# Score blocks of the recurrent stage: 32 by 32 diagonal pieces in place of whole 128 by 128 products

## The chip, the cores and the metric

The kernel runs on one core of a Trainium2 chip. Its time is the device time of one execution in microseconds (us). TensorE (PE in the profile, PEld for its weight loads) multiplies, VectorE (DVE), ScalarE (ACT) and GpSimd (POOL) do the rest, SyncE (SP) issues the transfers.

## The reference

One layer of an encoder: 1024 tokens and 16 meta tokens, width 1024. A projection feeds two branches, latent attention and a bidirectional gated recurrence (HGRN2, 8 heads of 128 channels); they are merged by gates, projected, and a SwiGLU feed-forward layer follows. The change lies in the recurrence. In short form, for one head and one direction, with the decays `g` summed up to `b` within a chunk:

```python
b = jnp.cumsum(g_c, axis=2)
q_r = q_c * exp(b - b_ref)            # b_ref: a reference point near the query
k_r = k_c * exp(b_ref - b)
a = einsum('td,sd->ts', q_r, k_r)     # scores inside the chunk
a = where(causal, a, 0.0)
o = a @ v_c + (q_c * exp(b)) @ S      # S: the state before the chunk
S = exp(b_last) * S + (k_c * exp(b_last - b)).T @ v_c
```

The reference point has to be near both positions, or the exponents grow too far. So the scores of a chunk are made in blocks, each with a reference of its own. Both directions are made and added.

## The kernel before

The stage of the recurrence, `hgrn_heads`, goes through the 8 heads. Its chunks have 128 tokens (`CH`), and it works on groups of 512 tokens (`HALF`, 4 chunks, `GC`). TensorE's program is software-pipelined: `project` makes the projections of the next head (13 outputs `e` of 8 steps `k` of three matmuls each, lines 88 to 90), and the list `PE_STEPS` says after which of these steps, numbered `e * 8 + k`, a piece of the current head's recurrence is put in:

```python
PE_STEPS = [(36, "turn", 0), (38, "turn", 1), (39, "updates", 0), (40, "turn", 2), (42, "updates", 1),
            (43, "turn", 3), (45, "turn", 4), (47, "updates", 2), (51, "inside", 0), (53, "updates", 3),
            (57, "updates", 4), (60, "inside", 1), (66, "outputs", 0), (71, "inside", 2), (75, "norm_sum", 0),
            (78, "inside", 3), (85, "outputs", 1), (90, "norm_sum", 1)]
```

ACT and DVE have such lists too (`ACT_STEPS`, `DVE_STEPS`). Every engine runs its own list in order, and semaphores tie them together. DVE's list has, in this order around the change: `factors_multiply` 0 (lines 822 and 825: the decay factors times queries and keys), `states` 2 (line 845), weight 3 (line 895), `factors_multiply` 1, `states` 3, `keep` 0, `factors_subtract` 2 (lines 797 to 802), `states` 4, `keep` 1, weight 4, `factors_subtract` 3, `factors_multiply` 2 and 3, `keep` 2.

`inside(h, i)` makes the scores of one direction and one group of 4 chunks, i = 0 to 3. It waits for `fac_done` (DVE's `factors_multiply` i) and for `kept` (DVE's `keep` i - 1 has read the bank), and writes `in_bank`, one PSUM bank of 128 partitions (keys) by 4 times 128 columns (queries):
- 4 matmuls of 128 by 128 (line 958), one for each chunk, with the factors `k32` and `q32`, whose references lie in the middle of every 32 tokens. Only the 32 by 32 blocks on the diagonal of these products are of use.
- 4 matmuls of 64 by 64 and 8 of 32 by 32 (line 967) for the blocks off the diagonal, which write over what the first 4 left there. For one direction the 64-wide ones all go to the same half of the partitions; the 32-wide ones go to partitions 0 and 64 in turn (forward) or 32 and 96 (backward).

The operands are fp32. Each such matmul stands in the trace as two pairs of a weight load and a matmul (two passes). `keep` then picks the valid triangle by a mask (`copy_predicated`). `updates` i waits for `ends_copied` and for `state_done` (DVE's `states` i - 1 has read the bank `u_bank`). The printed functions follow.

Of the kernel before, what the change touches and what calls it, by code (L numbers as in the profile page):

```python
# [43 lines left out]
CH = 128  # L44
NCH = SEQ // CH
SUB = 32
QUARTER = D // 4
HALF = 512
GC = HALF // CH
# [449 lines left out]
def hgrn_heads(nc, t, hn_hi, hn_lo, weights):  # L499
# [9 lines left out]
    with ExitStack() as c:  # L509
        def sb(name, shape, dt=F32):  # L510
            return c.enter_context(nc.sbuf_tensor(name, shape, dt))
# [5 lines left out]
        q, gate = sb("q", [P, SEQ]), sb("gate", [P, SEQ])  # L517
# [19 lines left out]
        ends_bank, in_bank, o_bank, u_bank = bank[4:8]  # L537
# [17 lines left out]
        zeroed, masks_filled, masks_made = t.sem("zeroed"), t.sem("masks_filled"), t.sem("masks_made")  # L555
# [21 lines left out]
        def place(dd, name, g=0):  # L577
            a = {"q64": 0, "k64": 256, "q128": 512, "k128": 768, "q32": 1024, "k32": 1536, "q0": 2048 + g * HALF}[name]
            n = 256 if name in ("q64", "k64", "q128", "k128") else HALF
            return factor[dd][:, a:a + n]  # L580
# [4 lines left out]
        with nc.Block() as block:  # L585
# [50 lines left out]
            def _(act):  # L636
                def sigmoids(h, _):

                    proj_copied.wait(act, h, N_PROJ)
                    q_done.wait(act, h, 1, lag=1)  # L640
                    kept.wait(act, h, 4, lag=1)
                    r_done.wait(act, h, 4, lag=1)
                    for n in IN_HGRN:
                        dst = {"q": q, "hg": gate}.get(n, raw[n])
                        act.activation(dst[:], raw[n][:], ACT.Sigmoid).then_inc(sig_done.sem, 1)
                    act.preload_act_table_set("natural_log_exp_and_others")
                    for dd, n in ((FWD, "ff"), (BWD, "fb")):
                        sig_done.wait(act, h, dd + 1)
                        hh = h.index() + dd * HEADS
                        act.activation(sub[dd][:], raw[n][:], ACT.Ln, bias=t.lb[:, bass.ds(hh, 1)],  # L650
                                       scale=t.omlb[:, bass.ds(hh, 1)]).then_inc(g_done.sem, 1)
# [85 lines left out]
            def _(dve):  # L737
# [150 lines left out]

                dve.wait_ge(masks_made, 1)
                dve.wait_ge(zeroed, 2)  # L890

                def weight_lo(p, s):

                    w_hi_done.wait(dve, p, s + 1)
                    dve.tensor_tensor(w_lo[s % 2][:], w_raw[s % 2][:], w_hi[s % 2][:].bitcast(F32),  # L895
                                      ALU.subtract).then_inc(w_lo_done.sem, 1)
# [16 lines left out]
            def _(pe):  # L913
# [34 lines left out]
                def inside(h, i):  # L948

                    dd, g = GROUPS[i]  # L950
                    fac_done.wait(pe, h, i + 1)
                    if i:
                        kept.wait(pe, h, i)
                    else:
                        kept.wait(pe, h, 4, lag=1)
                    for u in range(GC):
                        a = slice(u * CH, (u + 1) * CH)
                        pe.matmul(in_bank[:, a], place(dd, "k32")[:, a], place(dd, "q32")[:, a], start=True,
                                  stop=True)
                    for span in (128, 64):  # L960
                        half = span // 2
                        for n in range(HALF // span):
                            u, at = n * span // CH * CH, n * span % CH
                            keys = at + (0 if dd == FWD else half)
                            queries = u + at + (half if dd == FWD else 0)
                            b = slice(n * half, (n + 1) * half)
                            last = pe.matmul(in_bank[keys:keys + half, queries:queries + half],
                                             place(dd, f"k{span}")[:, b], place(dd, f"q{span}")[:, b],
                                             start=True, stop=True)
                    last.then_inc(in_done.sem, 1)  # L970

                def outputs(h, g):
# [22 lines left out]
                def project(p, h, s):  # L995

                    made = projections(p)
                    w_lo_done.wait(pe, p, s + 1)
                    for i, (a, w) in enumerate(made.chunks[s]):
                        e = made.first(s) + i  # L1000
                        same = [x for x in range(e) if made.banks[x] == made.banks[e]]
                        if same:
                            proj_copied.wait(pe, p, same[-1] + 1)
                        else:
                            last_use = max(x for x in range(N_PROJ) if OF_HEAD.banks[x] == made.banks[e])
                            proj_copied.wait(pe, p, last_use + 1, lag=1)
                        out = bank[made.banks[e]][:, 0:w]
                        for k in range(KT):
                            last = three(pe, out, w_hi[s % 2][:, k, :], w_lo[s % 2][:, k, :], hn_hi[:, k, a:a + w],
                                         hn_lo[:, k, a:a + w], k == 0, k == KT - 1)  # L1010
                            if k == KT - 1:
                                last.then_inc(proj_done.sem, 1)
                            if h is not None:
                                for at, name, j in PE_STEPS:
                                    if at == e * KT + k:
                                        steps[name](h, j)

                steps = {"turn": turn, "updates": updates, "inside": inside, "outputs": outputs,
                         "norm_sum": norm_sum}

                def both(p, h):
                    if h is not None and h.j is None and h.base == 0:
                        pe.wait_ge(zeroed, 2)
                    for s in range(6):
                        project(p, h, s)

                iterations(pe, both)


# [1958 lines left out]
```

## Time and profile before

| what | value |
|---|---|
| time of 3 runs | 2173.63, 2174.02 (median), 2174.09 us |
| span of the profiled execution, first to last instruction | 2171.4 us |
| what lies around the span (median minus span) | 2.6 us |
| stage of the recurrence | about 126 to 906 us of the span |
| calls of `inside` | 32 (8 heads by 4) |

The time that is compared is the one of the runs; stretches are read from the profiled execution, whose time is taken as its span and the 2.6 us around it. A matmul's duration in the trace is longer than its distance to the next one, since matmuls overlap: what a matmul costs is read from the distance of starts. Weight loads (PEld) overlap matmuls as well.

### The profile page before, as it was taken

The page shows a single profiled execution, that of the slowest core. Times are in us where ns is not written, and L with a number is a line of the kernel's source. Part 1 is how long each engine was busy: PE and PEld are TensorE (multiplying, and loading weights), DVE is VectorE, ACT ScalarE, POOL GpSimd, SP SyncE. Part 2 cuts the span into 40 slices and gives each one's busy share as a digit, 9 for nine tenths or more (in the row PEclk, how much of TensorE's full clock was granted, in tenths as well). Part 3 has the DMA queues.
Part 4 walks back from the last instruction along what each step waited for, and adds up shares of the span by engine and source line. Part 5 has one row for each costly group of instructions (what it writes and reads, how often), then busy time and mean ns, then how long its engine had stood idle before and what let it go on. Part 6 is the DMA issues. An engine that isn't in the chain of part 4 may idle for free. (4 is left out here: it accounts for less than half of the span.)

```text
span 2171.4 us, 30857 instructions
## 1 busy us (share of the span) xinstructions
PE 2124.8 (98%) x11536; PEld 1795.8 (83%) x11536; DVE 1282.6 (59%) x1966; ACT 948.0 (44%) x1550; POOL 397.9 (18%) x242
## 2 busy tenths in 40 slices
PE   8999999999999999999999999899999999999999
PEld 8988888888888888778888888777888888888886
DVE  3403664756647557447777777667866766651431
ACT  6314354443554535455555555545432323243422
POOL 1110000000000000021111111020065554524443
PEclk9999999999999999999999999999999999999999
DMA  5112111120120111130111111254322222354452
GB/s 188 60 54 69 35 64 53 45 68 34 63 68 34 63 52 46 49 138 1 45 45 48 47 50 47 99 186 159 135 83 81 95 78 73 124 182 165 149 182 96
DMA packets 79101, 181.82 MB, mean 84 GB/s; under 512 B 6976, under 2 KB 27776, under 8 KB 77344
## 3 DMA queue, kind: packets, MB, share of 16 engines
q1 hardware_dynamic: 79008, 180.56, 24.1%
q8 instruction: 61, 1.00, 0.2%
q14 instruction: 32, 0.26, 0.0%
HBM read 142.13 MB, written 38.40 MB: 83 GB/s over the span
## 5 line engine op out<-in xcount | busy, mean ns | idle before, releaser
L88 PE MATMUL h_bank<-hn_hi,w_hi 128*128 128x512 f32 (+2 forms) x952 | 371.1, 390 | 2.8 <-ACT raw L716 1.6
L90 PE MATMUL h_bank<-hn_hi,w_lo 128*128 128x512 f32 (+2 forms) x952 | 353.4, 371 | 0.0
L89 PE MATMUL h_bank<-hn_lo,w_hi 128*128 128x512 f32 (+2 forms) x952 | 353.0, 371 | 0.0
L88 PEld LDWEIGHTS h_bank<-hn_hi,w_hi 128*128 128x128 f32 x952 | 179.0, 188 | 33.3 <-issue 8.7
L90 PEld LDWEIGHTS h_bank<-hn_hi,w_lo 128*128 128x128 f32 x952 | 178.7, 188 | 27.9
L89 PEld LDWEIGHTS h_bank<-hn_lo,w_hi 128*128 128x128 f32 x952 | 179.2, 188 | 26.4 <-issue 3.8
L716 ACT COPY raw<-h_bank 128x512 f32<-128x512 f32 (+2 forms) x119 | 63.9, 543 | 279.9 <-PE h_bank L90 249.5
L2150 ACT CAST w_hi<-w_raw 128x1024 fp32r<-128x1024 f32 x79 | 82.8, 1049 | 213.2 <-PE f_bank L90 201.7
L895 DVE TENSOR_TENSOR w_lo<-w_raw,w_hi 128x1024 fp32r<-128x1024 f32 x52 | 63.5, 1221 | 138.2 <-ACT w_hi L696 138.2
L1132 POOL MEMSET ckv_hi<- 128x224 f32 x1 | 0.3, 284 | 778.8 <-POOLq L585 778.8
L1453 ACT CAST prob_hi<-a_bank 128x512 fp32r<-128x512 f32 x144 | 83.0, 588 | 130.8 <-PE a_bank L1721 130.2
L2120 POOL TENSOR_TENSOR w_lo<-w_raw,w_hi 128x1024 fp32r<-128x1024 f32 x45 | 108.3, 2406 | 144.5 <-ACT w_hi L2150 144.5
L88 PE MATMUL f_bank<-ffn_in_hi,w_hi 128*128 128x512 f32 x320 | 126.7, 396 | 2.1 <-DVE w_lo L2439 1.3
L90 PE MATMUL f_bank<-ffn_in_hi,w_lo 128*128 128x512 f32 x320 | 124.6, 389 | 0.0
L89 PE MATMUL f_bank<-ffn_in_lo,w_hi 128*128 128x512 f32 x320 | 124.5, 389 | 0.0
L2125 POOL TENSOR_TENSOR set_lo<-combos,set_hi 128x512 fp32r<-128x512 f32 x72 | 98.7, 1372 | 87.2 <-ACT set_hi L2213 87.2
L88 PE MATMUL f_bank<-t_hi,set_hi 128*128 128x512 f32 x288 | 112.0, 389 | 0.0
L89 PE MATMUL f_bank<-t_lo,set_hi 128*128 128x512 f32 x288 | 112.0, 389 | 0.0
L90 PE MATMUL f_bank<-t_hi,set_lo 128*128 128x512 f32 x288 | 112.0, 389 | 0.0
L1572 DVE TENSOR_TENSOR prob_lo<-a_bank,prob_hi 128x512 fp32r<-128x512 f32 x144 | 97.7, 688 | 24.0 <-ACT prob_hi L1453 20.3
L2213 ACT CAST set_hi<-combos 128x512 fp32r<-128x512 f32 x72 | 44.5, 618 | 99.8 <-PE f_bank L90 64.9
L88 PE MATMUL f_bank<-t_hi,w_hi 128*128 128x512 f32 x224 | 87.7, 391 | 0.0
(411 smaller groups left out, 5371.3 us busy)
## 6 DMA issues: line engine op xcount, KB each, us to landing
w_raw<-in_w_ffn SPq DMA_DIRECT2D x82, 512.0 KB, 3.7
w_raw<-in_w_hgrn SPq DMA_DIRECT2D x54, 512.0 KB, 3.2
raw_up<-in_w_ffn SPq DMA_DIRECT2D x18, 512.0 KB, 4.6
hidden<-gate_blocks SPq DMA_DIRECT2D x34, 256.0 KB, 2.0
w_raw<-in_w_out SPq DMA_DIRECT2D x15, 512.0 KB, 3.3
w_raw<-in_w_head SPq DMA_DIRECT2D x9, 512.0 KB, 6.0
X<-in_x SPq DMA_DIRECT2D x8, 520.0 KB, 9.4
values<-values_h SPq DMA_DIRECT2D x32, 128.0 KB, 1.7
```

The lines of the kernel that those rows point to most:

```text
L88: pe.matmul(out, wh, xh, start=start, stop=False)
L89: pe.matmul(out, wh, xl, start=False, stop=False)
L90: return pe.matmul(out, wl, xh, start=False, stop=stop)
L716: act.copy(t.raw[:, s * L + a:s * L + a + w], bank[made.banks[e]][:, 0:w]).then_inc(proj_copied.sem, 1)
L895: dve.tensor_tensor(w_lo[s % 2][:], w_raw[s % 2][:], w_hi[s % 2][:].bitcast(F32), ALU.subtract).then_inc(w_lo_done.sem, 1)
L1132: pool.memset(part[:, :, L:].bitcast(F32), 0.0).then_inc(padded, 1)
L1453: act.copy(turned_hi[k % RING][:], turn_bank[k % 2][:]).then_inc(p_hi.sem, 1)
L1572: dve.tensor_tensor(turned_lo[k % RING][:], turn_bank[k % 2][:], turned_hi[k % RING][:].bitcast(F32), ALU.subtract).then_inc(p_lo.sem, 1)
L2120: pool.tensor_tensor(w_lo[b % 2][:], w_raw[b % 2][:], w_hi[b % 2][:].bitcast(F32), ALU.subtract).then_inc(w_lo_done, 1)
L2125: pool.tensor_tensor(set_lo[:, i], product_source(mat, i), set_hi[:, i].bitcast(F32), ALU.subtract).then_inc(set_lo_done, 1)
L2150: act.copy(w_hi[b % 2][:], w_raw[b % 2][:]).then_inc(w_hi_done, 1)
L2213: act.copy(set_hi[:, i], product_source(mat, i)).then_inc(set_hi_done, 1)
```

## The change

The 4 whole products go. In their place, at the end of `inside`, stand 16 matmuls of 32 by 32 for the blocks on the diagonal; they go to partitions 0, 32, 64 and 96 in turn. The 4 matmuls of 64 by 64 and the 8 of 32 by 32 off the diagonal stay and come first, so a call of `inside` now issues 4 + 8 + 16 = 28 fp32 matmuls (56 passes) where it issued 4 + 4 + 8 = 16 (32 passes). The semaphore `in_done` is raised by the last of the 16. Blocks of the bank that nothing writes any more (below or above the diagonal) are set to zero once, by DVE, before the loop; TensorE waits for that before the first head of the recurrence.

```diff
                 dve.wait_ge(zeroed, 2)
+                dve.memset(in_bank[:], 0.0).then_inc(zeroed, 1)
...
-                    for u in range(GC):
-                        a = slice(u * CH, (u + 1) * CH)
-                        pe.matmul(in_bank[:, a], place(dd, "k32")[:, a], place(dd, "q32")[:, a], start=True,
-                                  stop=True)
                     for span in (128, 64):
                         half = span // 2
...
-                            last = pe.matmul(in_bank[keys:keys + half, queries:queries + half],
-                                             place(dd, f"k{span}")[:, b], place(dd, f"q{span}")[:, b],
-                                             start=True, stop=True)
+                            pe.matmul(in_bank[keys:keys + half, queries:queries + half],
+                                      place(dd, f"k{span}")[:, b], place(dd, f"q{span}")[:, b],
+                                      start=True, stop=True)
+                    for n in range(HALF // SUB):
+                        at, b = n * SUB % CH, slice(n * SUB, (n + 1) * SUB)
+                        last = pe.matmul(in_bank[at:at + SUB, b], place(dd, "k32")[:, b], place(dd, "q32")[:, b],
+                                         start=True, stop=True)
                     last.then_inc(in_done.sem, 1)
...
-                        pe.wait_ge(zeroed, 2)
+                        pe.wait_ge(zeroed, 3)
```

## Rows read from the trace of the kernel before

**Rows 1.** The page: span, busy time of the engines, share, instructions.

```profile
span 2171.4 us, 30857 instructions
PE 2124.8 (98%) x11536; PEld 1795.8 (83%) x11536; DVE 1282.6 (59%) x1966; ACT 948.0 (44%) x1550; POOL 397.9 (18%) x242
```

**Rows 2.** Recurrence stage: length, busy PE, PEld, DVE, ACT, POOL, granted clock, DMA.

```profile
126.00:906.00 780.00, 775.40 (x4712) 662.23 (x4712) 446.27 (x780) 343.48 (x499) 1.68 (x4) 1.00 0.16 52
```

**Rows 3.** TensorE's waits over the span: who for whom, total us, times, longest.

```profile
PE h_bank L958 <- DVE factor_f L825: 1.9, 8, 0.3
```

**Rows 4.** Timeline of TensorE around `inside` 1, second head: start, length, instruction.

```profile
326.72 0.39 PE L90 MATMUL h_bank<-hn_hi,w_lo 128*128 128x512 f32 x1
326.95 1.05 PE L958 MATMUL h_bank<-factor_b 128*128 128x128 f32 x8
327.93 1.05 PE L967 MATMUL h_bank<-factor_b 128*64 128x64 f32 x24
328.92 0.50 PE L88 MATMUL h_bank<-hn_hi,w_hi 128*128 128x512 f32 x1
329.25 0.39 PE L89 MATMUL h_bank<-hn_lo,w_hi 128*128 128x512 f32 x1
```

**Rows 5.** The same call in narrow windows: last whole pass, 64-wide, 32-wide passes.

```profile
327.73 0.28 PE L958 MATMUL h_bank<-factor_b 128*128 128x128 f32 x1
...
327.93 0.68 PE L967 MATMUL h_bank<-factor_b 128*64 128x64 f32 x8
...
328.54 0.45 PE L967 MATMUL h_bank<-factor_b 128*32 128x32 f32 x16
```

**Rows 6.** Groups by line and form, 220 to 890 us: busy us, mean ns.

```profile
L967 PE MATMUL h_bank<-factor_b 128*64 128x64 f32 x128 | 10.9, 228 | 0.0
...
L967 PE MATMUL h_bank<-factor_b 128*32 128x32 f32 x256 | 7.1, 199 | 0.0
```

**Rows 7.** Timeline of DVE and TensorE around `inside` 0, second head.

```profile
316.08 0.68 DVE L825 TENSOR_TENSOR factor_f<-factor_f,key_f 128x512 f32<-128x512 f32 x1
...
316.81 1.16 PE L958 MATMUL h_bank<-factor_f 128*128 128x128 f32 x8 [0.26 <-DVE factor_f L825]
...
317.90 1.05 PE L967 MATMUL h_bank<-factor_f 128*64 128x64 f32 x24
...
318.88 0.50 PE L88 MATMUL h_bank<-hn_hi,w_hi 128*128 128x512 f32 x1
```

**Rows 8.** Timeline of DVE from weight 3 to `keep` 0, second head.

```profile
317.70 1.22 DVE L895 TENSOR_TENSOR w_lo<-w_raw,w_hi 128x1024 fp32r<-128x1024 f32 x1
...
321.38 0.68 DVE L825 TENSOR_TENSOR factor_b<-factor_b,key_b 128x512 f32<-128x512 f32 x1
321.98 1.49 DVE L845 SCALAR_TENSOR_TENSOR state<-state,decay,h_bank 128x128 f32<-128x128 f32 x4
323.40 0.75 DVE L876 COPY_PREDICATED scores<-consts,h_bank 128x512 f32<-128x512 uint32 x1
```

**Rows 9.** Timeline of the weight loads: the first load of `updates` 4.

```profile
323.78 0.19 PEld L944 LDWEIGHTS h_bank<-values_h,ends_t 128*128 128x128 f32 x1
```

**Rows 10.** ACT's copy before `updates` 2; TensorE's sequencer at line 83 in 310.36:310.70.

```profile
309.75 0.59 ACT L665 COPY ends_t<-h_bank 128x512 f32<-128x512 f32 x1 [1.39 <-PE h_bank L927]
...
L83 PEldq ALU_OP  x1: 32/32/32, 310.4 to 310.4; - x1
```

**Rows 11.** Timelines of DVE, ACT and TensorE between `inside` 1 and `inside` 2.

```profile
329.12 0.06 DVE L864 MEMSET waited<- 128x1 f32 x1 [2.04 <-PE h_bank L967]
...
331.29 0.59 ACT L716 COPY raw<-h_bank 128x512 f32<-128x512 f32 x1 [6.91 <-PE h_bank L90]
...
336.98 0.69 DVE L825 TENSOR_TENSOR factor_f<-factor_f,key_f 128x512 f32<-128x512 f32 x1
...
339.23 0.49 PE L958 MATMUL h_bank<-factor_f 128*128 128x128 f32 x3
```

**Rows 12.** Timeline of DVE: its first instruction of the stage.

```profile
138.93 1.22 DVE L895 TENSOR_TENSOR w_lo<-w_raw,w_hi 128x1024 fp32r<-128x1024 f32 x1 [44.52 <-ACT w_hi L696]
```

## The prediction, made before the changed kernel was run

> **What bounds the kernel now.** The page comes first: TensorE is busy 98% of the span, DVE 59%, ACT 44% [rows 1]. Then the stage of the recurrence by itself: TensorE is busy 775.4 of 780 us at a granted clock of 1.00, which is the level of 2.4 GHz [rows 2]. So time comes off only where TensorE's own work shrinks, and only as long as nobody else becomes late. The list of waits shows who is nearly late: `inside` 0 of each head waits for DVE's `factors_multiply` 0, 8 times, 1.9 us in all [rows 3]. Busy time is no price here, because neighbours on TensorE overlap; prices come from distances between starts in the timeline. I read them in one head; the groups have one mean duration over the stage [rows 6].
>
> **One call of inside, now.** In `inside` 1 the first whole product starts at 326.95 and the projection goes on at 328.92: 1.97 us. The starts split it into 0.98 (8 passes of whole products), 0.61 (8 passes 64 wide) and 0.38 (16 passes 32 wide) [rows 4, 5]. Subtracting one duration from the end of a group gives its last start:
> - whole products: last start 327.73, so (327.73 - 326.95) / 7 = 0.111 a pass, then 0.20 to the first 64-wide start;
> - 64 wide: end 328.61, less 0.22 is 328.39, so 0.46 / 7 = 0.066 a pass, then 0.15;
> - 32 wide: end 328.99, less 0.20 is 328.79, so 0.25 / 15 = 0.0167 a pass, then 0.13 [rows 5, 6].
>
> The 0.20, 0.15 and 0.13 are stops at a change of the matmul's form.
>
> **Removed.** The 8 whole passes with their stop, 0.98 us. A new stop takes their place, from the projection's 512 columns to the 64-wide form. No row shows it. After a whole pass 0.20 go by, of which its 128 columns stream for 0.05 at 2.4 GHz; 0.15 follow the stream. A projection matmul streams 512 columns in 0.21, and the next one starts 0.23 after it [rows 4]. So the stop adds 0.21 + 0.15 - 0.23 = about 0.13; I take 0.135, with 0 (hidden) and 0.20 (the whole distance) as its bounds.
>
> **Added.** 16 matmuls, 32 passes, 32 wide, behind the 16 passes of that form that stay. No further change of form. What counts is their pace, and whether it is that of the 16 old ones depends on where they go. The 64-wide matmuls of one call all go to one half of the partitions and take 0.066 a pass. The 32-wide ones alternate between two column groups. Half the columns should take half of that, 0.033; the row has 0.0167 [rows 5]. I read this as two groups working side by side, each at 0.033 a pass. The new ones go round four groups. If four work side by side, groups 0 and 64 (or 32 and 96) have 16 passes each, 8 old and 8 new, and set the end: 15 x 0.033 + 0.02 for the stagger of the groups = 0.52 from first to last start. I take this, as the nearest reading of the rows. If only two ever work side by side, it is 47 x 0.0167 = 0.785.
>
> By the Trainium skill (TensorEngine Tiling (Array Packing), Key Properties) different tiles load weights and multiply in parallel; this supports four, and would give the 0.52. The trace shows two. The same notes speak against the change elsewhere: TensorE: Matmul & The Clock Gate, section "Wait — 56ns, not 53.3ns?", says that start to start is never below about 25 ns, however few the columns. The trace has 17 ns over 16 passes; whether it holds over 48 no row shows, and that is a rival below.
>
> Can the sequencer issue so many? Behind the wait of `turn` 4, which ACT's copy ends at 309.75 + 0.59 = 310.34, stand 20 weight loads and matmuls (`turn` 4 and two steps), then the wait of `updates` 2, whose sequencer operation is there at 310.4 [rows 10]: 0.1 us at most for 20, 5 ns each. 48 passes are 96 instructions, 0.48 us, under the 0.52. So issue doesn't bind, though with little to spare.
>
> **A call of inside, after.** 0.135 + 0.61 + 0.52 + 0.13 = 1.395 us, so 1.97 - 1.395 = 0.575 saved in `inside` 1, 2 and 3.
>
> **Inside 0 is different.** There the engine is idle before it, so no stop at the front: from 316.81 to 318.88 are 2.07 now [rows 7], after it 0.61 + 0.52 + 0.13 = 1.26, 0.81 saved. But it can't be kept. `updates` 4, six steps later, waits for `states` 3. DVE works without a gap from `factors_multiply` 0 through weight 3, `factors_multiply` 1 and `states` 3, which ends at 321.98 + 1.49 = 323.47 [rows 8]. It doesn't wait for TensorE in that stretch, so it won't be earlier. TensorE's first load of `updates` 4 is at 323.78 [rows 9]; a load follows DVE's end by about 0.05 (316.76 to 316.81, [rows 7]), so it could be at 323.52. Of the 0.81, 0.26 are kept and 0.55 become a wait at `updates` 4. The wait before `inside` 0 stays at 0.26: what leads to it is unchanged.
>
> **Is anything else late after that?** TensorE reaches `inside` 2 earlier by 0.26 + 0.575 = 0.84. Its factors are ready at 336.98 + 0.69 = 337.67, its first product starts at 339.23 with the load 0.23 ahead: 1.3 to spare [rows 11]. And that DVE work moves along: DVE sits idle until `inside` 1 ends, and ACT's copy is released by the projection [rows 11]. So the rest is kept.
>
> **The rest.** The memset on DVE is one instruction of 128 x 512, priced by the nearest row on the same bank at 0.75 [rows 8]; DVE is idle until 138.93, for 44.52 us [rows 12]: nothing. Without that cover it would be 0.75 once. The wait for `zeroed` comes a head later: nothing.
>
> **The sum.** A head gives 0.26 + 3 x 0.575 = 1.985, 8 heads 15.9 us. The profiled execution is 2171.4 + 2.6 = 2174.0, the median of the runs. 2174.0 - 15.9 = 2158.1.
>
> **Rivals.**
> - *Two groups at a time.* For it: it is the only pace in the rows. Against: nothing in them says that two is the limit. A call takes 0.135 + 0.61 + 0.785 + 0.13 = 1.66, saves 0.31; `inside` 0 would save 0.545, keeps 0.26. A head: 1.19, in all 9.5: 2164.5.
> - *A slower pace in a long burst.* The short burst of now may live on what is already queued, and a longer one fall to a slower pace. I price it half way between the 0.0167 of two groups and the 0.033 of one, at 0.025 for the new passes: 0.25 + 32 x 0.025 + 0.13 = 1.18; a call 1.925, saves 0.045; a head 0.26 + 3 x 0.045 = 0.395, in all 3.2: 2170.8, no change that a measurement tells. Against: the 5 ns of issue. The 25 ns of the Trainium skill (TensorE: Matmul & The Clock Gate, the section named above) would come to this.
> - *Neighbouring groups don't overlap* (slower). The rows show only groups two apart, 0 and 64 or 32 and 96; the new order takes 0, 32, 64, 96. If each pass has to wait for its neighbour: 0.25 + 32 x 0.033 + 0.13 = 1.436; a call 2.18, loses 0.21; `inside` 0 keeps 0.02. A head loses 0.61, in all 4.9: 2178.9. It decides from the pace at which a head breaks even: three calls may lose 0.087 each, so 32 passes may take 1.97 + 0.087 - 0.745 - 0.38 = 0.93, 0.029 a pass. At the 0.066 of the 64-wide ones it would be over 30 us slower.
> - *Everything is given back*: TensorE waits elsewhere, DVE or ACT setting the length of a head. For it: DVE already holds two places in each head. Against: the 1.3 us at `inside` 2, and that DVE is released by TensorE there. It gives 2174.
>
> **How the numbers follow.** Four side by side 0.55, two 0.23, the slower pace 0.08, no overlap of neighbours or worse 0.10, all given back 0.04. The forecast is the first, 2158. The first two hold 0.78, so the range reaches to the third, 2171. Its low end: with the stop at the front hidden, 3 x 0.135 x 8 = 3.2 less, 2154.9, and a little of what I let be lost at `updates` 4; 2154. A measurement of this kernel tells 0.2%, 4.3 us, from no change: 2169.7 and 2178.4. So faster 0.78, same 0.12 (slower pace and all given back), slower 0.10.
>
> **What would show it.** Right: line 958 is gone; the 32-wide group of a call takes about 0.5 us from first to last start; a call lasts about 1.4; the waits show `updates` 4 (line 944) waiting for DVE's line 845, about 0.5 us in each head, and nothing new before `inside` 1 to 3; granted clock stays 1.00. Wrong: 32-wide starts 0.025 or 0.033 apart; a stop between old and new 32-wide ones; or a stop at the front beyond 0.20. The pace of the new passes is the step most likely to fail.

## The result, and the profile after

The changed kernel takes 2158.15 us (2157.74 to 2158.28); the kernel before took 2174.06 beside it. The ratio is 0.9926, with a 95% interval of 0.9912 to 0.9939: 0.7% less, which is small but clear of the noise. The prediction was 2158.0, range 2154 to 2171. The number is met; the parts below show that two of its terms were off and that a third, unforeseen cost made up for them. Times are medians; one execution of the last version below took 10,700 us at a granted clock of 0.18, and its time is given without it.

The page of the kernel after, which answers to [rows 1]: span, busy time, instructions.

```profile
span 2156.3 us, 32394 instructions
PE 2108.2 (98%) x12304; PEld 1771.7 (82%) x12304; DVE 1283.3 (60%) x1967; ACT 948.1 (44%) x1550; POOL 397.3 (18%) x242
```

The stage of the recurrence, as in [rows 2], from its first matmul to the end of its last:

```profile
126.69:888.82 762.13, 756.20 (x5480) 637.50 (x5480) 445.86 (x781) 343.52 (x498) 1.64 (x4) 1.00 0.16 53
```

It was 779.8 us long from its first matmul (126.09) to the end of its last (905.91) and is 762.1 now: 17.7 less, at the same granted clock of 1.00. The span is only 15.1 shorter (2171.4 less 2156.3). So 2.6 us were lost outside the stage; they come up again below.

TensorE's timeline around `inside` 1 of the second head, which answers to [rows 4]. The projection before the call ends in the first line, and it resumes in the last but one.

```profile
324.76 0.39 PE L90 MATMUL h_bank<-hn_hi,w_lo 128*128 128x512 f32 x1
325.08 0.96 PE L964 MATMUL h_bank<-factor_b 128*64 128x64 f32 x18
325.85 0.22 PE L969 MATMUL h_bank<-factor_b 128*32 128x32 f32 x1
325.87 0.23 PE L964 MATMUL h_bank<-factor_b 128*32 128x32 f32 x3
325.90 0.22 PE L969 MATMUL h_bank<-factor_b 128*32 128x32 f32 x2
...
325.96 0.45 PE L969 MATMUL h_bank<-factor_b 128*32 128x32 f32 x28
326.34 0.50 PE L88 MATMUL h_bank<-hn_hi,w_hi 128*128 128x512 f32 x1
326.67 0.40 PE L89 MATMUL h_bank<-hn_lo,w_hi 128*128 128x512 f32 x1
```

And in a narrow window, as in [rows 5], the first of the 32-wide passes:

```profile
325.69 0.29 PE L964 MATMUL h_bank<-factor_b 128*32 128x32 f32 x6
```

Three things are to be seen. From the last projection matmul to the next one are 326.34 - 324.76 = 1.58 us, where it was 328.92 - 326.72 = 2.20 [rows 4]: 0.62 saved. The 48 passes 32 wide run from 325.69 to 325.96 + 0.45 - 0.20 = 326.21: 0.52 us for 47 steps, 0.011 a pass. And the first new matmuls (line 969) start between old ones (line 964) that stand ahead of them in the program, so they didn't wait for all of the old ones.

The same for `inside` 0, with its wait in brackets, and the place where `updates` 4 begins; they answer to [rows 7] and [rows 9]:

```profile
315.21 1.02 PE L964 MATMUL h_bank<-factor_f 128*64 128x64 f32 x21 [0.22 <-DVE factor_f L825]
...
316.47 0.50 PE L88 MATMUL h_bank<-hn_hi,w_hi 128*128 128x512 f32 x1
...
321.36 0.39 PE L90 MATMUL h_bank<-hn_hi,w_lo 128*128 128x512 f32 x1
321.92 1.16 PE L945 MATMUL h_bank<-values_h,ends_t 128*128 128x128 f32 x8 [0.17 <-DVE state L845]
322.83 0.48 PE L88 MATMUL h_bank<-hn_hi,w_hi 128*128 128x512 f32 x1
```

TensorE's waits, as in [rows 3]: the second line and the third are new. The third belongs to the feed-forward part.

```profile
PE h_bank L964 <- DVE factor_f L825: 1.9, 8, 0.3
...
PE h_bank L945 <- DVE state L845: 1.5, 8, 0.3
...
PE f_bank L88 <- POOL w_lo L2121: 0.9, 1, 0.9
```

DVE's `states` 3 in the same head, as in [rows 8]:

```profile
320.38 1.49 DVE L845 SCALAR_TENSOR_TENSOR state<-state,decay,h_bank 128x128 f32<-128x128 f32 x4
```

It ends at 321.87, and `updates` 4 (line 945 now) starts at 321.92. The list gives this wait 1.5 us in all, 0.19 a head, since a matmul's modelled end covers part of it; what it costs is seen in the starts. Matching the projection's matmuls of the two kernels one by one (the nth of line 88 with the nth), the changed kernel's TensorE gains 0.78 to 0.84 us at `inside` 0, loses 0.42 to 0.50 again at `updates` 4, and gains 0.59 to 0.62 at each of `inside` 1 to 3. In the second head the last two are 0.44 and 3 x 0.62.

### The profile page after: what moved, and what is told of

Same layout as the page of the kernel before. It is cut to its first block and busy times, and to the rows that moved or that the text cites. A ratio compares the mean times of both kernels' runs of the same rounds, so it can differ in the third digit from the quotient of the medians.

```text
span 2156.3 us, 32394 instructions
## 1 busy us (share of the span) xinstructions
PE 2108.2 (98%) x12304; PEld 1771.7 (82%) x12304; DVE 1283.3 (60%) x1967; ACT 948.1 (44%) x1550; POOL 397.3 (18%) x242
## 3 DMA queue, kind: packets, MB, share of 16 engines
q8 instruction: 63, 1.03, 0.2%
```

## The experiments

A column group is here the set of 32 partitions of the PSUM bank (0, 32, 64 or 96 and the 31 behind it) to which a 32-wide matmul writes. Where one time is given, the kernel ran once; the kernel before, beside it, took 2173.34 us with the first three, 2174.33 (median of seven) with the order by chunk and the three better versions, and 2174.02 with the last two. The executions of one kernel scatter by 1 to 2 us, so small differences are read from stretches of the trace and not from these times.

**Do column groups work side by side?** Three kernels send the 16 new matmuls of a call elsewhere. They multiply the factors `k64` and `q64`, so that the bank holds bounded numbers; the scores on the diagonal are left out. The first sends all to one group:

```diff
-    at, b = n * SUB % CH, slice(n * SUB, (n + 1) * SUB)
-    last = pe.matmul(in_bank[at:at + SUB, b], place(dd, "k32")[:, b], place(dd, "q32")[:, b],
+    at, b, c = 0, slice(n * SUB, (n + 1) * SUB), slice(n % 8 * SUB, (n % 8 + 1) * SUB)
+    last = pe.matmul(in_bank[at:at + SUB, b], place(dd, "k64")[:, c], place(dd, "q64")[:, c],
```

> The 16 new matmuls of a call all write partitions 0 to 31, with the factors k64 and q64 in place of k32 and q32, so the blocks on the diagonal are not computed. Theory (column groups work side by side, each at about 0.032 us a pass): forward calls have 8 + 32 = 40 passes in group 0, 1.27 us from the first to the last 32-wide start, instead of 0.52; backward calls 32 there, 1.0 to 1.3 us. A head gets 2.1 to 2.6 us longer (0.43 of inside 0 is taken up by the wait at updates 4), the kernel 17 to 21: 2175 to 2179. Rival (a pace by the number of instructions, wherever they go): 0.52 us as now, 2158.

The others have `at = n % 2 * 64` and `at = n % 2 * SUB`.

> The 16 new matmuls go to partitions 0 and 64 in turn (factors k64 and q64, blocks on the diagonal not computed). Theory (each group 0.032 us a pass): forward calls have 24 passes in each of two groups, 0.76 us from first to last 32-wide start; backward calls, whose old ones go to 32 and 96, between 0.52 (old and new side by side) and 0.76. 2160 to 2164. Rival (pace by number): 0.52, 2158.

> The 16 new matmuls go to the neighbours 0 and 32 in turn (factors k64 and q64, blocks on the diagonal not computed). Theory: neighbours overlap like groups two apart, forward 24 passes in group 0, 0.76 us, 2160 to 2164, as with 0 and 64. Rival (neighbours share a path): 0.25 + 32 x 0.033 = 1.3 us, about 2176.

They took 2176.40, 2161.19 and 2161.84 us, all three as the theory has it. The timelines of `inside` 0 in the second head, all to one group:

```profile
317.90 1.05 PE L964 MATMUL h_bank<-factor_f 128*64 128x64 f32 x24 [0.26 <-DVE factor_f L825]
318.79 1.18 PE L969 MATMUL h_bank<-factor_f 128*32 128x32 f32 x32
319.89 0.50 PE L88 MATMUL h_bank<-hn_hi,w_hi 128*128 128x512 f32 x1
```

and in turn to groups 0 and 64:

```profile
315.19 1.05 PE L964 MATMUL h_bank<-factor_f 128*64 128x64 f32 x24 [0.26 <-DVE factor_f L825]
316.07 0.68 PE L969 MATMUL h_bank<-factor_f 128*32 128x32 f32 x32
316.68 0.50 PE L88 MATMUL h_bank<-hn_hi,w_hi 128*128 128x512 f32 x1
```

The calls take 1.99 and 1.49 us, where the changed kernel's takes 1.26. Less 0.61 in front and 0.13 behind, the 32-wide part is 1.25, 0.75 and 0.52: for 40, 24 and 16 passes in the busiest group that is 1.25 / 39 = 0.032 a pass, 0.75 / 23 = 0.033, and 0.52 / 15 = 0.035 with the stagger of the groups in it. So in these forward calls the busiest group sets the end, at one pace. With the neighbours 0 and 32 a call takes 1.48 in both directions, 24 passes in the busiest group again, so neighbours overlap like groups two apart. The rival of a pace by number falls, and so does the one in which neighbours share a path.

The backward calls show a limit. There the old 32-wide matmuls go to 32 and 96, and in the second kernel the new ones go to 0 and 64, which are free. No group has more than 16 passes, yet the part takes 0.66 us and not 0.52. Its `inside` 1 in the second head:

```profile
325.07 0.96 PE L964 MATMUL h_bank<-factor_b 128*64 128x64 f32 x18
325.84 0.22 PE L969 MATMUL h_bank<-factor_b 128*32 128x32 f32 x2
...
325.93 0.61 PE L969 MATMUL h_bank<-factor_b 128*32 128x32 f32 x27
326.47 0.50 PE L88 MATMUL h_bank<-hn_hi,w_hi 128*128 128x512 f32 x1
```

By the single starts in the trace, the call's first 32-wide pass is at 325.68. The first new one follows at 325.84, 0.16 later, when 10 of the 16 old passes have started. From there 16 passes a group at 0.032 make up the rest. With all new ones in group 0 the backward part takes 1.16: 0.16 and 31 x 0.032. So TensorE looks ahead in its program only part of the way, and a free group does not help before the work for it comes near. In the changed kernel this costs nothing, since its new matmuls go to all four groups in turn.

**Does a change of form cost a stop?** The same 28 matmuls, ordered by chunk: one 64 wide, its two off the diagonal, its four on it; four times. `block` is the body of the old loop.

```diff
-    for span in (128, 64):
-        for n in range(HALF // span):
-            ...
-    for n in range(HALF // SUB):
+    for u in range(GC):
+        block(128, u)
+        block(64, 2 * u)
+        block(64, 2 * u + 1)
+        for n in range(4 * u, 4 * u + 4):
             ...
```

> The same 28 matmuls of a call as in the changed kernel, ordered by chunk: one of 64, then the 6 of 32 of the same 128 tokens, four times. Theory (each change of form is a stop of 0.13 to 0.15 us from the last start): 6 more changes and four short groups, a call 0.8 to 1.0 us longer, of which inside 0 loses 0.43 less: 2180 to 2188. Rival (the gaps are the tail of a group of matmuls and don't come from the form): 2158 to 2162.

2180.07 us. TensorE's timeline of `inside` 1, its first half; line 963 is a call of `block`:

```profile
327.41 0.48 PE L963 MATMUL h_bank<-factor_b 128*64 128x64 f32 x4
327.68 0.23 PE L973 MATMUL h_bank<-factor_b 128*32 128x32 f32 x2
...
327.73 0.25 PE L973 MATMUL h_bank<-factor_b 128*32 128x32 f32 x6
327.91 0.48 PE L963 MATMUL h_bank<-factor_b 128*64 128x64 f32 x4
...
329.43 0.50 PE L88 MATMUL h_bank<-hn_hi,w_hi 128*128 128x512 f32 x1
```

The call takes 329.43 - 327.41 = 2.02 us and not 1.26, with the same matmuls. The last start of the first 32-wide group is 327.73 + 0.25 - 0.20 = 327.78, and the next 64-wide one comes at 327.91: 0.13, and in the trace 0.15 go by from the last 64-wide start to the first 32-wide one, each four times a call. Six more changes for 0.77 us are 0.13 a change. The kernel is slower than before the change. So the order by form is part of why the change pays.

**Is it DVE's states 3 that takes back what inside 0 saves?**

```diff
-            (57, "updates", 4), (60, "inside", 1),
+            (58, "updates", 4), (60, "inside", 1),
```

> The changed kernel with updates 4 one projection step later (after step 58, not 57), nothing else. Theory (DVE's states 3 gives back 0.43 us of each head at updates 4): the wait of line 945 for DVE's line 845 goes, TensorE keeps the 0.43, 8 heads 3.4 us: 2154.7. Rival (DVE or ACT would hold TensorE somewhere else in the head anyway): the wait moves to inside 1 or inside 2 and the time stays at 2158. On the second finding, a weight load of the feed-forward part that takes 7.0 us and not 5.7 in the four kernels with the longer program, where a 16 KB load of instructions runs beside it: TensorE's program here has as many instructions as in the changed kernel, so the wait of about 1 us for POOL's w_lo stays.

2153.65 us (2152.51 to 2154.22, four executions), ratio to before 0.9903 (0.9887 to 0.9920). The wait for line 845 is gone from the list, no wait of the stage took its place, and the stage takes 758.5 us, 3.6 less. The rival falls. The other half of the expectation holds too: the wait of 1.0 us for POOL's `w_lo` is still there.

**More of the same, as a better version?** The 64 by 64 blocks become two matmuls each, of 32 keys by 64 queries:

```diff
-    pe.matmul(in_bank[keys:keys + half, queries:queries + half],
-              place(dd, f"k{span}")[:, b], place(dd, f"q{span}")[:, b],
-              start=True, stop=True)
+    for c in range(0, half, SUB):
+        pe.matmul(in_bank[keys + c:keys + c + SUB, queries:queries + half],
+                  place(dd, f"k{span}")[:, n * half + c:n * half + c + SUB],
+                  place(dd, f"q{span}")[:, b], start=True, stop=True)
```

> The changed kernel with each 64 by 64 block made as two matmuls of 32 keys by 64 queries, so that a call has one narrow form only: 64 passes 32 wide in place of 8 of 64 and 48 of 32. Theory (column groups side by side at 0.032 a pass, a stop at every change of form): group 0 has the most passes in a forward call, 24, so 23 x 0.032 + 0.02 = 0.75 us from first to last start, a call about 1.0 with its stops, where it is 1.35; inside 1 to 3 save 0.35 each, inside 0 gives its saving to the wait at updates 4: 8.4 us, 2149.7. Rival (64 columns streamed by each pass hold up the groups, or the pace falls with 64 passes in a row): 2158 or more. The longer program moves the loads of instructions by a part of a block: if they matter, the 1 us wait for POOL's w_lo in the feed-forward part is gone or stands elsewhere.

2152.27 us (2151.53 to 2153.33, four executions), ratio 0.9899 (0.9883 to 0.9916). `inside` 1, its first 4 and its first 11 passes in narrow windows (the eleventh already streams 32 columns), and its end:

```profile
323.76 0.30 PE L965 MATMUL h_bank<-factor_b 128*32 128x64 f32 x4
...
323.76 0.48 PE L965 MATMUL h_bank<-factor_b 128*32 128x64 f32 x11
...
324.84 0.50 PE L88 MATMUL h_bank<-hn_hi,w_hi 128*128 128x512 f32 x1
```

A call takes 1.08 us where I had reckoned 0.9 without the stop in front; it was 1.26. The direction was right, the size half, and the rival's reason is the one that the trace bears out: 64 streamed columns do hold up the groups, though not by so much that the gain goes. From the 4th start, 323.76 + 0.30 - 0.22, to the 11th, 323.76 + 0.48 - 0.22, are 0.18 for 7 passes: 0.026 a pass. These passes alternate between only two groups, so a group takes 0.05 to 0.06 a pass (0.056 from start to start in the trace), where a pass of 32 columns takes 0.032; the 64-wide weights with 64 columns took 0.058. Eight such passes in the busiest group, 0.024 longer each, are 0.19 a call, and that closes the account: from first to last start 0.95 us, where 0.75 was expected. In three calls of each of 8 heads it is 4.6 us, and the stage gains 4.0 and not 8.4. The trace has no stop inside the 32-wide part where 64 columns give way to 32; the greatest distance of two starts there is 0.055. So the stop at a change of form goes with the width of the weights, not with the columns streamed.

With it and `updates` 4 after step 59:

> Both: all blocks 32 keys wide, and updates 4 after step 59. Theory: the 0.35 saved in inside 0 is now kept too, and so are the 0.43: 2149.7 less 8 x 0.78 = 6.2, 2143.5. Rival (something else becomes late, inside 1 behind keep 0 first): between 2144 and 2150, with a wait at line 964.

2147.81 us (2147.45 to 2149.04, three executions), ratio 0.9879 (0.9860 to 0.9899). It is the fastest of all and 26 us under the kernel before, but 4 over what I expected. The stage takes 753.4 us, 4.8 less than with `updates` 4 at step 57; no wait of line 845 is left and none came at `inside` 1, as the rival would have it. What is missing is again the pace with 64 columns: 0.19 in each of 32 calls is 6.1 us, of which 1.3 us come back in the feed-forward part, for a reason that the next experiments show.

**Where do 2.6 us go outside the stage?** First the kernel before, once more:

> The kernel before, profiled once more: it is to show how much of the 17.7 us gained in the stage of the recurrence, of which only 15.1 are left at the end of the span, is given back by something that the change causes. If the 2.6 us are scatter of starts and transfers between executions, the first matmul of the stage and the time from the end of the stage to the end of the span differ between the two profiles of the kernel before by amounts of that size (0.5 to 2 us). If the change causes it, the two profiles of before agree within 0.3 us there.

It took 2173.79 us. Its stage takes 779.84 us, the first time 779.82. The start of the stage scatters: 125.3 in this profile, 126.1 in the first, 126.7 in the changed kernel. So does attention: 439.8, 438.8 and 439.0. The feed-forward part doesn't: 780.7 and 780.4 in the two profiles of before, 782.3 in the changed kernel, and 782.0 to 782.4 in the five others with as many instructions. So of the 2.6 us, 0.6 are the later start and 1.8 the feed-forward part. I followed the latter to one place. It is a transfer of 512 KB of weights from memory (not a weight load of TensorE). These are, in the changed kernel's timelines, its issue by SP, the cast that waits for it, and the wait of TensorE that follows:

```profile
1979.92 10.95 SPq L1968 DMA_DIRECT2D w_raw<-in_w_ffn  x3
...
1986.96 1.05 ACT L2151 CAST w_hi<-w_raw 128x1024 fp32r<-128x1024 f32 x1 [5.64 <-DMA w_raw<-in_w_ffn]
...
1990.61 0.47 PE L88 MATMUL f_bank<-t_hi,w_hi 128*128 128x512 f32 x1 [0.91 <-POOL w_lo L2121]
```

And its DMA queues from 1979.9 to 1987 (packets, MB, share of 16 engines):

```profile
q1 hardware_dynamic: 411, 2.04, 81.8%
q8 instruction: 1, 0.02, 0.9%
```

The transfer lands 7.0 us after its issue; in the kernel before it takes 5.7. ACT, POOL and TensorE follow it. Beside it, in q8, stands one packet of 16 KB of instructions, which the kernel before has at another time. TensorE's program has 576 instructions more in its text (48 in each of 4 calls, in three copies of the loop's body). The Trainium skill (Runtime: NRT & Kernel Launch, section "Instruction fetch mechanics") has engines fetch their program in blocks of 16 KB, 256 instructions; the packet of 0.02 MB fits that, and 576 is two such blocks and 64, so the borders of all later ones would move by 64. Two kernels test it. The first gives the kernel before 64 more, the second the changed kernel 192 more:

```diff
+    for n in range(16):                      # 48 in the second
+        at = n * SUB % P
+        pe.matmul(bank[0][at:at + SUB, 0:SUB], t.const("ones")[:, 0:SUB], t.const("ones")[:, 0:SUB],
+                  start=True, stop=True)
     for n, tiles in (("ckv", KVT), ("cq", QT)):
```

> The kernel before with 16 small fp32 matmuls (32 columns) added at the start of TensorE's program of the next stage, where it waits for ACT anyway: 64 instructions more. The changed kernel has 576 more in its text, which is 64 beyond two whole loads of 256 (16 KB at 64 bytes). Theory (a load of instructions beside a weight load costs about 1 us in the feed-forward part): with these 64 the kernel before gets the changed kernel's phase; a 16 KB load stands beside the weight load issued near 1996, which takes 7.0 us and not 5.7, and TensorE waits about 1 us for POOL's w_lo; the feed-forward part takes 782 us and not 780.5. Rival (it comes from the recurrence's new timing): 780.5, no such wait.

> The changed kernel with 48 such small matmuls at the same place: 192 instructions more, 768 in all against the kernel before, three whole loads, so the phase of before. Theory: the wait of about 1 us for POOL's w_lo is gone and the feed-forward part takes about 780.7 us, not 782.3; the 48 matmuls cost at most 0.8 us, mostly under the wait for ACT. Rival: the wait stays.

The first took 2175.52 us beside 2174.02 of the kernel before: the transfer takes 7.0 us, a packet of instructions starts beside it at 2001.6, the feed-forward part takes 781.8. The second took 2157.39: the transfer takes 5.7, the packet stands at 1992.5, the wait is gone and the feed-forward part takes 781.0. TensorE's waits of the first:

```profile
PE f_bank L88 <- POOL w_lo L2124: 0.9, 1, 0.9
```

So the wait comes and goes with the place of the instruction load, and 1.1 to 1.4 us with it; 0.3 to 0.5 of the 1.8 stay unexplained, since the second kernel's 781.0 is not quite the 780.4 to 780.7 of before. The two versions with all blocks narrow have 768 instructions more, three whole loads, and the feed-forward part takes 781.0 and 780.9 there.

Other transfers show the same. Counted through the 100 weight transfers of the feed-forward part, the fourth takes 5.0 and 4.6 us in the changed kernel and in the first of these two, where a packet of instructions starts 1.0 us after its issue; in both profiles of before and in the second kernel no packet stands beside it, and it takes 3.1 to 3.2. The last takes 4.6 and 5.9 us with a packet and 3.1 to 3.2 without. It isn't so for every packet: one that starts just as a transfer is issued leaves it at 3.3 us in the changed kernel, where it takes 3.1 to 3.2 without. TensorE waits only where a transfer has no time to spare. The packet itself took 0.97 us; how it holds up the others isn't shown.

## Why the prediction was right, and where it wasn't

- *A call, 32-wide part.* Predicted 0.52 us from four groups side by side, measured 0.52. This was the step I held most likely to fail. The reading of the 16 old passes as two groups at a time was right, and the experiments show its rule: 0.032 a pass in each group. That the number came out so well is partly luck. The 0.066 of the 64-wide passes is a mean that holds one long first distance: in the trace 0.107 from the first to the second start, then 0.058. Half of 0.058 is 0.029, not 0.033.
- *A call, stop in front.* Taken as 0.135, measured 0.09: 325.08 - 324.76 = 0.32, less the 0.23 from one projection matmul to the next. The step that failed is "its 128 columns stream for 0.05 at 2.4 GHz". These are fp32 passes. The prediction's own 0.111 from one whole pass to the next spoke against 0.05, and a row that I had not used shows what they stream at. It is TensorE's timeline of the kernel before at `norm_sum` 0:

```profile
344.05 1.02 PE L992 MATMUL h_bank<-o_square,consts 128*128 128x512 f32 x2
```

Two fp32 passes of 512 columns, each 0.59 long (the group of line 992 in the grouped instructions: 590 to 592 ns), so their starts lie 1.02 - 0.59 = 0.43 apart: 0.84 ns a column, about twice what the projection's fp32r takes, with 0.23 us for 512 columns. A whole pass of 128 columns streams for 0.107, 0.20 - 0.107 = 0.09 follow it, and 0.21 + 0.09 - 0.23 = 0.07 would have been the term. The 0.045 less in three calls of each head made the stage 1.0 us faster than predicted.
- *Inside 0.* Predicted 0.81 saved in the call, measured 2.07 - 1.26 = 0.81.
- *Updates 4.* The wait was foreseen with its place and its cause, and the first load starts where it was put, 0.05 behind DVE. The size was off: I took 0.55 as lost; 0.42 to 0.50 were, 0.44 in the second head. I compared the starts of the first weight load. But from that load to the next projection matmul went 324.81 - 323.78 = 1.03 us before, where the load ran beside the last projection matmul, and go 322.83 - 321.92 = 0.91 now, where nothing runs beside it. So the loss, read from the next projection matmul, is about 0.11 smaller. That gives 0.9 us more over 8 heads. Before, that matmul was this one:

```profile
324.81 0.48 PE L88 MATMUL h_bank<-hn_hi,w_hi 128*128 128x512 f32 x1
```

- *The rest of the head.* No other wait came, as predicted; DVE and ACT moved along.
- *The sum.* A head was to give 1.985 us and gives 0.81 - 0.44 + 3 x 0.62 = 2.23; 8 heads 17.8, and the stage is 17.7 shorter. That is 1.9 us more than predicted, the 1.0 and the 0.9 above. The forecast of 15.9 agrees with the measured 15.9 because 1.8 us were lost in the feed-forward part, most of them at one weight transfer, which I had not thought of, and some tenths to the scatter of the start. It was right in its mechanisms for the stage and closer in its number than it had earned: that part is luck.
- *The rivals.* Two at a time: refuted by 0.52 us for 48 passes. A slower pace in a long burst: refuted up to 64 passes in a row, where those of 32 columns still come 0.032 apart in a group. Neighbours: refuted. All given back: refuted, only `inside` 0 gave some back. The memset cost nothing that shows: one DVE instruction more (1967 for 1966) and no wait.

What sets the pace of a group can be read from three forms. After the first pass of a form, passes of 128, 64 and 32 fp32 columns start 0.111, 0.058 and 0.032 us apart; at 0.84 ns a column they stream for 0.107, 0.054 and 0.027. And 64 columns through weights 32 wide instead of 64 take 0.056 for 0.058. So the columns streamed set it, and the width of the weights hardly does. What the 2 to 5 ns on top are stays open, and so does how many instructions the sequencer could still feed.

## What to carry to other kernels

On TensorE a small product is not cheap because it is small. A whole 128 by 128 product in fp32 is two passes, 0.22 us here. Its four 32 by 32 blocks are eight passes: sent through one column group they take as long, 8 x 0.032 = 0.26 us, and spread over four groups a quarter of that. So count the passes of the busiest column group and the changes of form, not the matmuls. Go round the groups in turn, so that work for a free group is never far ahead in the program, and put matmuls of one form together. When work moves off the engine that is the bound, look in its order for the next wait on another engine: here one step in the hand-written order took back 0.44 us of each head until `updates` 4 was moved by one step.

## What the runs showed of the hardware

- Four column groups of 32 work at the same time, neighbours too, each at 0.032 us an fp32 pass of 32 columns; 48 passes in 0.52 us are 0.011 from start to start. The Trainium skill (TensorE: Matmul & The Clock Gate, section "Wait — 56ns, not 53.3ns?") gives about 25 ns as the least distance of starts. Within one group the 32 ns agree with that; across groups the measurement decides against it.
- A matmul that is later in the program can start before an earlier one of another column group: line 969 at 325.85, line 964 at 325.87. The same page of the Trainium skill (section "The mechanism") has matmuls start and end strictly in program order; here the trace disagrees.
- This looking ahead ends somewhere: with groups 0 and 64 free in a backward call, the first matmul for them started 0.16 us after the first of the 16 passes ahead of it, when 10 of these had started.
- A change between 64-wide and 32-wide weights costs 0.13 us; the same 28 matmuls took 2.02 us with seven changes inside the call and 1.26 with one.
- A load of 16 KB of instructions on a queue of its own can lengthen a transfer of 512 KB of weights from memory by 1 to 2 us where both fall together (7.0 for 5.7 us, 5.0 for 3.2), so an edit at one place of a long program can cost a microsecond at another, a millisecond later.
